# State-space stage: the second G table earlier, rotations in its scratch, and another order of ScalarE's queue and of the DMA queue

## What is computed

```python
def s5_mixer(h, w_in, lam_re, lam_im, log_step, b_re, b_im, c_re, c_im, d_skip, w_glu):
    u = (h @ w_in).reshape(bsz, seq, SSM_GROUPS, SSM_GROUP)
    step = exp(log_step)[:, None]
    a = exp((lr + i * li) * step)                  # complex decay of each state
    b = ((a - 1) / (lr + i * li)) * (b_re + i * b_im)
    x[l] = a * x[l - 1] + b @ u[l]                 # a scan over the sequence, per group
    y[l] = real(c @ x[l]) + d_skip * u[l]
    z = gelu(y)
    val, gate = split(z @ w_glu)
    return val * sigmoid(gate)
```

## Time and profile before

| | us |
|---|---|
| median of 3 runs | 1895.33 (1894.39 to 1896.41) |
| the profiled execution | 1895.86 |
| its span (first to last instruction) | 1894.1 |
| PE busy in the span | 1825.6 (96%) |
| VectorE, ScalarE, GpSimd busy | 1051.8, 834.4, 191.8 |

### The profile page before, as it was taken

The page is one execution under the profiler, slowest core; times in us unless marked ns, Lnnn a source line. Parts: engine busy times, 40 slices in busy tenths (PEclk is TensorE's granted clock), DMA queues, the critical chain, the costliest instruction groups (busy, mean ns, idle before and its releaser), DMA issues.

```text
span 1894.1 us, 24279 instructions
## 1 busy us (share of the span) xinstructions
PE 1825.6 (96%) x8908; PEld 1415.8 (75%) x8908; DVE 1051.8 (56%) x1622; ACT 834.4 (44%) x1400; POOL 191.8 (10%) x261
## 2 busy tenths in 40 slices
PE   7789999999999999999999999989999999999997
PEld 5677878888888766667888888868766777866675
DVE  8594454444433767766444434466464566555647
ACT  5132344344222666744444422233466633356753
POOL 7950000000000000000000000023000102200000
PEclk9779999999999999999999999999999999999999
DMA  6212223222333210112322333323111122311111
GB/s 217 74 38 72 89 90 100 99 91 98 92 99 99 70 34 27 61 57 89 100 92 96 100 92 92 106 74 106 67 56 49 53 78 85 105 56 56 55 41 61
DMA packets 58763, 152.19 MB, mean 80 GB/s; under 512 B 17152, under 2 KB 22048, under 8 KB 58672
## 3 DMA queue, kind: packets, MB, share of 16 engines
q1 hardware_dynamic: 55120, 148.27, 24.5%
q0 software_dynamic: 3552, 2.70, 0.5%
HBM read 143.79 MB, written 4.19 MB: 78 GB/s over the span
## 4 chain that ended last, share of the span: by engine, by line
PE 86%; POOL 4%; DVE 3%; ACT 3%; issue 1%; SPq 1%; DMA 0%; DVEq 0%; ACTq 0%; POOLq 0%
PE bank L1974 18%; PE bank L1975 18%; PE bank L1976 18%; PE bank L2462 3%; PE bank L2464 3%; PE bank L2463 3%; PE bank L2439 2%; PE bank L2427 2%; PE bank L2426 2%; PE bank L2425 2%; PE bank L2194 1%; PE bank L2222 1%; PE bank L2549 1%; PE bank L2477 1%; PE bank L2446 1%
## 5 line engine op out<-in xcount | busy, mean ns | idle before, releaser
L1203 DVE TENSOR_TENSOR wl<-raw,wh 128x1024 fp32r<-128x1024 f32 (+3 forms) x280 | 323.6, 1156 | 495.1 <-ACT wh L645 492.0
L645 ACT ACTIVATE wh<-raw 128x1024 fp32r<-128x1024 f32 (+3 forms) x280 | 279.1, 997 | 592.8 <-PE bank L1976 516.8
L1974 PE MATMUL bank<-xH,wh 128*128 128x512 f32 x904 | 355.9, 394 | 12.5 <-DVE wl L1203 10.6
L1975 PE MATMUL bank<-xL,wh 128*128 128x512 f32 x904 | 353.1, 391 | 0.0
L1976 PE MATMUL bank<-xH,wl 128*128 128x512 f32 x904 | 353.0, 390 | 0.0
L1974 PEld LDWEIGHTS bank<-xH,wh 128*128 128x128 f32 x904 | 170.6, 189 | 51.1 <-DVE wl L1203 10.2
L1975 PEld LDWEIGHTS bank<-xL,wh 128*128 128x128 f32 x904 | 170.6, 189 | 35.8 <-issue 1.0
L1976 PEld LDWEIGHTS bank<-xH,wl 128*128 128x128 f32 x904 | 170.4, 188 | 35.8
L1974 PE MATMUL bank<-hidH,wh 128*128 128x512 f32 x352 | 137.4, 390 | 0.0
L1975 PE MATMUL bank<-hidL,wh 128*128 128x512 f32 x352 | 137.0, 389 | 0.0
L1976 PE MATMUL bank<-hidH,wl 128*128 128x512 f32 x352 | 137.0, 389 | 0.0
(11 more groups left out here) (449 smaller groups left out, 3335.8 us busy)
## 6 DMA issues: line engine op xcount, KB each, us to landing
raw<-w_gu_dram SPq DMA_DIRECT2D x88, 512.0 KB, 3.3
raw<-w_p_dram SPq DMA_DIRECT2D x64, 512.0 KB, 3.3
raw<-w_dn_dram SPq DMA_DIRECT2D x32, 448.0 KB, 3.3
raw<-w_glu_dram SPq DMA_DIRECT2D x16, 512.0 KB, 3.6
raw<-w_dn_dram SPq DMA_DIRECT2D x16, 512.0 KB, 3.5
raw<-w_out_dram SPq DMA_DIRECT2D x16, 512.0 KB, 3.3
raw<-w_in_dram SPq DMA_DIRECT2D x8, 512.0 KB, 7.8
raw<-w_o_dram SPq DMA_DIRECT2D x8, 512.0 KB, 3.2
```

The costliest lines, as they stand in the source:

```text
L645: nc.scalar.activation(wh[:, (st.base + u) % 2, 0:kts * P], raw[:, (st.base + u) % 4, 0:kts * P], ACT.Copy).then_inc(w_high, 1)
L1203: nc.vector.tensor_tensor(wl[:, s, 0:kts * P], raw[:, (st.base + u) % 4, 0:kts * P], wh[:, s, 0:kts * P].bitcast(F32), ALU.subtract).then_ ...
L1974: nc.tensor.matmul(bank, wh[:, s, w], hi[:, k, :], start=first and kt == 0, stop=False)
L1975: nc.tensor.matmul(bank, wh[:, s, w], lo[:, k, :], start=False, stop=False)
```

## The change

- rotr and roti, the scratch of the rotations, are the two halves of tv and no longer lie over xH.
- VectorE: `make_g(1)` moves ahead of input 5, `last_phases` behind it (and behind the split of block 7); input 7 is taken inside pass q = 0, behind the rotations, and VectorE zeroes the first columns of rho and state there. The splits of w_glu blocks 0 and 1 move to the end of pass q = 2.
- GpSimd no longer fills rho, state and MS with zeros, nor waits for the inputs.
- ScalarE fills all of MS with zeros and works in the order rho(0), WM, fill, `copy_lags(0)`, rho(1), high part of w_glu block 1.
- SyncE: `mat_shift(q + 1)` comes before `read_u(q + 2)`, which waits for `outputs(q)` (`toeplitz_used`) instead of `y_ready`.
- PE: `from_g(1, (0, 1))` comes before `states(0)` and block 7; `from_g(1, (2, 3))` before `lags(1)`; `lags(1)` doesn't wait for `lag_ready` any more. Five matmuls on zeros run at the start of the kernel.

```diff
-    rotr = core.tensor("rotr", [P, QP, NCH])
-    roti = core.tensor("roti", [P, QP, NCH])
+    rotr, roti = (tv[:, ri * QP * NCH:(ri + 1) * QP * NCH].rearrange("p (a b) -> p a b", a=QP) for ri in range(2))
...
-            for q in range(NQ):
-                mat_shift(q)
+            mat_shift(0)
+            for q in range(NQ - 1):
+                mat_shift(q + 1)
                 if q + 2 < NQ:
-                    sp.wait_ge(sem("y_ready"), q + 1)
+                    sp.wait_ge(sem("toeplitz_used"), q + 1)
                     read_u(q + 2)
...
-            pool.wait_ge(sem("u_ready"), KD)
-            step(nc.gpsimd.memset(rho[:, :, :, 0:1], 0.0))
-            step(nc.gpsimd.memset(state[:, :, :, 0:1], 0.0))
-            step(nc.gpsimd.memset(MS[:, :, :, :], 0.0))
-            pool.sem_inc(sem("pool_tables"), 1)
...
             next_block(6)
-            next_block(7)
-            copy_w(1, (0, 1))
...
-            act.wait_ge(sem("pool_tables"), 2)
+            copy_w(1, (0, 1))
+            act.wait_ge(sem("phases_ready"), 1)
+            act.wait_ge(w_used, st.base + KD - 1 + 3)
+            decay_rows(0)
+            copy_w(1, (2, 3))
+            step(nc.scalar.activation(MS[:, :, :, :].rearrange("p l g k -> p (l g k)"), tiny[:, 2:3].to_broadcast([P, CH * QG * GK]), ACT.Copy))
             copy_lags(0)
-            copy_w(1, (2, 3))
-            act.wait_ge(sem("phases_ready"), 1)
-            decay_rows(0)
             decay_rows(1)
+            next_block(7)
...
             take_input(4)
-            last_phases()
+            make_g(1)
             take_input(5)
             next_block(5)
-            make_g(1)
+            last_phases()
             take_input(6)
-            next_block(6)
-            take_input(7)
...
                 if q:
                     turned_low(q - 1)
+                else:
+                    take_input(KD - 1)
+                    step(nc.vector.memset(rho[:, :, :, 0:1], 0.0))
+                    step(nc.vector.memset(state[:, :, :, 0:1], 0.0))
...
-                if q == 0:
-                    next_block(KD - 1)
                 if q + 2 < NQ:
                     make_g(q + 2)
+                elif q + 2 == NQ:
+                    next_block(KD - 2)
+                    next_block(KD - 1)
...
             def lags(q):
-                if q:
+                if q >= 2:
                     pe.wait_ge(sem("lag_ready"), q)
...
             st = stages["w_in"]
+            pe.wait_ge(sem("tiny_ready"), 1)
+            for _ in range(5):
+                nc.tensor.matmul(banks[5][0:64, :], tiny[:, :], tiny[:, 2:3].to_broadcast([P, S]), start=True, stop=True)
...
                     if n == 7:
+                        from_g(1, (0, 1))
                         states(0)
...
-            from_g(1, (0, 1))
+            from_g(1, (2, 3))
             lags(1)
-            from_g(1, (2, 3))
             outputs(0)
```

## The result

| | before | after |
|---|---|---|
| median, us | 1895.09 (1894.39 to 1896.41, 4 runs) | 1879.69 (1877.17 to 1882.77, 4 runs) |
| the profiled execution | 1895.86 | 1881.66 |
| its span | 1894.1 | 1879.8 |
| start of w_glu's first dense product | 178.08 | 165.85 |

The ratio is 0.9919 (95% interval 0.9900 to 0.9938). The time forecast was 1880.2 and 15.1 us of gain; 15.4 were measured. The changed kernel scatters more than the old one: 6.9 us between its ends, against 3.1 us for all runs of the kernel before that stood beside these (1893.32 to 1896.41).

The account below looks back on a forecast made before the run. PE bounds the kernel, waiting before 176 us at four kinds of place (second G table, `lags(1)`, `states(1)`, shifted MS copies), its clock lowered. Gains 13.2 + 0.3 + 1.6 = 15.1 us give 1880.2 us, range 1875.5 to 1886.8.

Parts of the forecast that it names:

- The first term: Work up to `outputs(0)`: it starts at 89.7 us instead of 95.8, a gain of 6.1 us.
- Warm-up: Kernel start: zero matmuls bring `from_g(0)` 1.0 us sooner; block 5's end unchanged (bounds 1.2 us sooner, 0.9 later).
- `last_phases`: VectorE before the last input: three operations at 2.82, 8.5 us (bounds 3.7 and 8.5); `take_input(7)` ends at 77.5.
- rival B: VectorE wins nothing up to the last input; `outputs(0)` at 93.8, gain 11.0 us, time 1884.3; chance 0.24.
- The DMA queue: From the last input through the read of U(1) and the shift: `outputs(0)` starts 12.2 us behind `take_input(7)`.
- The scan and `states(1)`: Behind `outputs(0)`: scan done near 85, `states(1)` without wait in 2.2 us; 4.6 us of idle time, 1.5 and 1.0 of clock.
- The pass q = 1: The 1.83 us shift wait goes, but the hole before `from_g(3)` gets about 2.4 us; gain 0.3 (0 to 1.8).
- The pass q = 2: `outputs(2)` starts right behind `lags(3)`, without its wait for the shift; gain 1.6 us (0 to 1.6).
- After 176 us: Dense blocks to the end: order and waits unchanged, gain 0; any move other than the shift would show error.
- C: `last_phases` costs 3.7 to 5 us, `take_input(7)` follows block 7 at once: 3.8 us more gain, 1876.4; chance 0.16.
- D: PE's clock stays low through passes q=1 and q=2: 17 us lost, time 1897.2; chance 0.04.
- E: A queue order makes a new wait (ScalarE's fill or U(2) late), leaving 0 to 3.7 us: 1893; chance 0.04.

Follow-up runs that it names:

- e6: Changed kernel plus two more matmuls on zeros ahead of `from_g(0)`, where PE had waited; 1879.47 us, ratio 0.9916.
- e1: Changed kernel without the five warm-up matmuls on zeros; 1880.34 us, ratio 0.9920.
- e8: Kernel before the change plus only the five warm-up matmuls on zeros; 1895.07 us, ratio 1.0000.
- e2: Changed kernel with `take_input(7)` ahead of the six rotations of q = 0 instead of behind them; 1879.28 us, ratio 0.9920.
- e5: Changed kernel with VectorE's old order: `last_phases` ahead of input 5, `make_g(1)` behind the split of block 7; 1890.13 us, ratio 0.9976.
- e12: Changed kernel with MS zero-filled by GpSimd again, behind `make_v(0)` and the last input, instead of by ScalarE; 1881.42 us, ratio 0.9926.
- e9: Changed kernel with two more matmuls on zeros ahead of `from_g(0)` and `take_input(7)` ahead of all six rotations; 1877.77 us, ratio 0.9911.
- e14: Changed kernel plus one VectorE copy from a PSUM bank ahead of `make_g(3)` in the pass q = 1; 1884.70 us, ratio 0.9952.
- e4: Changed kernel with SyncE's old order: shifts, wait for `y_ready`, read of U, next shifts; 1884.25 us, ratio 0.9948.
- e13: Changed kernel without the warm-up matmuls and with `take_input(7)` behind the first two rotations of q = 0; 1876.79 us, ratio 0.9903.

## Why the prediction was right or wrong

The time and its sign came out as forecast, and the mechanism was the one named: the waits at the four kinds of place removed, one longer wait for the shift's DMA in their stead. The first term did not: the prediction calls its size wrong if `take_input(7)` ends off by over 2 us, and it ended 3.7 us late. Step by step:

- *Warm-up.* Its first half was right (block 0 at the high speed, `from_g(0)` near 45.6 behind 2 us of idle time; it was 46.2 and 1.95). The bound behind it failed: I let block 5 end at most 0.9 us later. By ScalarE's next step it ended 2.9 us later (62.97 against the 60.10 of the earlier trace rows), since all of `lags(0)` ran at the low clock: 7.04 us where it had taken 3.76. (The transposes behind it ran slowly in both kernels, 1.95 and 1.93 us.) I had charged a part of it only: my own two prices, 7.04 and 4.32, less the 1.0 us of the earlier start, already give 1.7 us, and the start was earlier by 0.35 us. e6, with the clock up and `last_phases` at 6.9 us, meets the term; e1, with `lags(0)` at 3.76 us but `last_phases` at 9.2, gets input 7 to 79.9 only, so that both misses count. e8 shows that the low clock costs nothing in the kernel before. Why the clock falls there stays open between the idle time and the thin work.
- *`last_phases`.* 8.5 us were taken for it, at the upper bound of the rows; it took 9.3 (3.41 + 2.94 + 2.93). The choice between its two prices was right for this execution. In e2 and e6 VectorE came early enough to wait 1.19 and 0.52 us for GpSimd's tables; then the first operation took 1.23 us, as in the earlier trace rows, and the three 6.9. With block 5 this puts `take_input(7)` at 81.2 instead of 77.5, outside the bounds of 73.6 and 79. It is rival B's place for that input, with B's start of `outputs(0)` at 93.8 (measured 93.5). The term for `outputs(0)` was 6.1 and measured 2.3.
- *The DMA queue.* 12.2 us from the last input to `outputs(0)`: measured 12.3 in the changed kernel, 12.2 to 12.3 in e2, e5 and e12, and 12.5 in e9. The fill was hidden, as said; e12 shows that its move to ScalarE is worth nothing here.
- *The scan and `states(1)`.* 7.1 forecast, 6.7 measured. The wait is gone; `states(1)` took 2.89 us and not 2.20, as the clock rose later behind `outputs(0)`.
- *The pass q = 1.* 0.3 forecast, 2.3 measured. The step that failed is that the hole before `from_g(3)` "gets about 2.4": it kept the 9.1 us of `make_g(3)`, which took 7.2. VectorE had been behind GpSimd, which began its own operation 0.35 us sooner:

```profile
123.84 2.02 POOL L504 TENSOR_TENSOR tp<-Cz,pw 128x1024 f32<-128x1024 f32 x1
```

After the change it came 0.4 us earlier relative to GpSimd (I had reckoned 0.3 and not what it sets off), was first, and won 1.5 us on the first operation alone. e14 shows it: 0.7 us of delay gives 2.3 back. So PE's hole before `from_g(3)` was 1.0 us.

- *The pass q = 2.* 1.6 forecast, 0.9 measured: the wait is gone, and `states(3)` ran at a lower clock, 2.8 us. e4 puts the two passes' DMA order together at 3.3 us of rest, where I had 1.9. A hole before `from_g(3)` that is smaller than reckoned, and so absorbs less, accounts for about that much; no run tests this by itself.
- *After 176 us.* I called any other difference than the shift a sign of error. There is one, 2.0 us, and it is in two places. In the 20 us around PE's 5 us wait for the layer norm near 1240 (4.97 and 4.96 us) the clock was granted at 0.83 in one and at 0.91 in the other:

```profile
1234.00:1254.00 20.00, 15.03 (x46) 8.07 (x46) 16.25 (x24) 9.77 (x14) 4.76 (x5) 0.83 0.15 52
```

```profile
1221.70:1241.70 20.00, 15.04 (x52) 8.10 (x51) 16.20 (x24) 9.77 (x14) 4.76 (x5) 0.91 0.16 52
```

That is the kernel before, then the changed one, 20 us each over the same work; some 1.2 us come from here and 0.8 from a like place some 320 us later. Of the kernels that start from the changed one, e5, e9 and e14 show 0.83 here, and from w_glu's first product to the end they took 1716.7 to 1717.4 us; the other eight show 0.91 like the changed one, with 1715.7 to 1716.3 us. So the change alone doesn't set it. The profile of the kernel before and that of e8 both have 0.83, and no profile shows the kernel before at 0.91. But of its 38 runs beside the experiments 18 had a mean granted clock of 0.979 to 0.982 and a median of 1895.4 us, the other 20 one of 0.983 to 0.987 and 1894.1 us: it has a like difference of its own, and the medians hold a part of it that I can't separate.

- *The rivals.* At `outputs(0)` B was right and the forecast wrong, and the terms that B keeps behind it came as it says. C's price for `last_phases` (3.7 to 5 us) was not met: 9.3, and still 6.9 in e6. D, a low clock through both passes, didn't come: stretches of 99 to 119 and 119 to 138 us had 0.91 and 0.82. E's new waits didn't come.

The right total is thus partly luck: 3.8 us too much at `outputs(0)`, 0.4 and 0.7 too much behind it, 2.0 too little in the pass q = 1 and 2.0 that lie in the clock of the rest.

## What to carry to other kernels

When an engine is let ahead, ask what it will then wait for: here a warm-up bought 2 us, turned them into an idle stretch, and in the profiled executions `lags(0)` lost 3.3 us to the clock behind it. Where a DMA chain hangs on the last of several inputs, take that input as soon as it is there and put the hidden work behind it; one line of order gave 3 us (e13 against e1: 3.6). And where two engines compete for the same port, their order of arrival can be worth more than the work moved: 0.4 us here decided over 2 us.

## What the runs showed of the hardware

- `lags(0)`, the same 32 matmuls in every kernel, took 3.76 us behind 0.84 us or less of idle PE (five profiles), 5.72 to 7.04 us behind 1.93 to 2.23 us (six), and 3.76, 4.85 and 5.22 us where matmuls on zeros filled the gap. The granted clock goes with it (0.50 against 1.00 in the stretch from 50 to 56 us of the changed kernel and e6). It is not steady for the same instructions: e2, e4, e5, e12 and e14 leave PE's list up to `lags(0)` as in the changed kernel, and have 3.76, 5.72, 3.76, 7.04 and 5.76 us.
- This place alone is 3.3 us of the 7 us by which the end of block 6 differs between the profiles. That it is also behind the spread of the other runs is argued from e1 and not shown.
- The clock can fall with PE busy throughout: 1.00 from 44 to 50 us and 0.54 from 50 to 56 in e9, no idle time in either.
- Five matmuls on zeros, with 64 output columns, brought the first real matmuls from 0.43 to 0.23 us apart. The granted clock of the profile doesn't show this start: in the kernel before it reads 1.00 from 9.7 to 13.7 us, where the matmuls are 0.43 us apart.
- A two-input SBUF operation of VectorE that meets one of GpSimd waits for its end: 1.23 us became 2.43 to 3.41; and the other way round 2.03 us became 3.04.
